# Two transformer blocks on one core: the first block's down-projection turned to token rows with 512 columns, and twelve products of constants ahead of the second up-projection

## The reference, cut to what matters

```python
def first_block(x, ...):
    ...
    x = x + mixed @ w_out[l]
    u = _rmsnorm(x, g_mlp[l]) @ w_ff1[l]
    x = x + jnp.square(jax.nn.relu(u)) @ w_ff2[l]      # 4096 -> 1024
    return x

def second_block(x, ...):
    u = rmsnorm(h, norm_mix_pre_w[layer])
    proj = u @ w_in[layer]                             # q, k, v first
    ...
    h = h + rmsnorm(mixed, norm_mix_post_w[layer])
    f = rmsnorm(h, norm_ffn_pre_w[layer])
    f = jnp.square(jax.nn.relu(f @ w_up[layer])) @ w_down[layer]
    h = h + rmsnorm(f, norm_ffn_post_w[layer])
    return h
```

## Time and profile before

| | |
|---|---|
| runs of the kernel before | 1190.92 us, three times the same |
| the profiled execution's own time | 1192.29 us |
| its span, first to last instruction | 1190.5 us |
| TensorE (PE) busy | 99% of the span |
| VectorE (DVE) busy | 70% |
| ScalarE (ACT) busy | 56% |
| GpSimdE (POOL) busy | 1% |
| mean granted TensorE clock | 0.998 |
| read from memory | 210.87 MB, 178 GB/s over the span |

### The profile page before, as it was taken

The page is one execution under the profiler, slowest core; times in us unless marked ns, Lnnn a source line. Parts: engine busy times, 40 slices in busy tenths (PEclk is TensorE's granted clock), DMA queues, the critical chain, the costliest instruction groups (busy, mean ns, idle before and its releaser), DMA issues.

```text
span 1190.5 us, 19559 instructions
## 1 busy us (share of the span) xinstructions
PE 1179.1 (99%) x8398; PEld 1105.6 (93%) x8398; DVE 829.2 (70%) x952; ACT 664.2 (56%) x766; POOL 16.4 (1%) x34
## 2 busy tenths in 40 slices
PE   9999999999999999999999999999999999999998
PEld 8999999999888899999999999999988888999886
DVE  7867676787756567776547758999987557677543
ACT  7543545677553445544434558889885435555342
POOL 0000000000000000000000000000000000000000
PEclk9999999999999999999999999999999999999999
DMA  9553445556665645556564746556456644555651
GB/s 328 166 172 108 148 146 166 152 159 182 212 218 192 207 148 165 189 178 213 177 186 153 233 123 202 179 172 197 162 191 234 205 149 160 167 173 186 219 204 43
DMA packets 181269, 213.23 MB, mean 179 GB/s; under 512 B 6700, under 2 KB 147372, under 8 KB 181184
## 3 DMA queue, kind: packets, MB, share of 16 engines
q1 hardware_dynamic: 177696, 200.30, 52.5%
q0 software_dynamic: 2912, 10.79, 3.0%
q10 hardware_dynamic: 576, 0.90, 0.2%
HBM read 210.87 MB, written 1.09 MB: 178 GB/s over the span
## 4 chain that ended last, share of the span: by engine, by line
PE 87%; DVE 9%; ACT 3%; issue 1%; DMA 0%; DVEq 0%; ACTq 0%
PE ps L242 50%; PE ps L2013 20%; PE ps L2342 7%; PE ps L1764 5%; DVE w_lo L210 3%; DVE arena L1270 3%; PE ps L1813 1%; PE ps L1767 1%; ACT w_hi L204 1%; DVE arena L1593 1%; PE ps L2302 1%; DMA pcol<-in_params 0%; DVE arena L1609 0%; PE ps L2309 0%; DVE arena L1625 0%
## 5 line engine op out<-in xcount | busy, mean ns | idle before, releaser
L210 DVE TENSOR_TENSOR w_lo<-raw,w_hi 128x2048 fp32r<-128x2048 f32 x187 | 428.0, 2290 | 195.6 <-ACT w_hi L204 195.3
L242 PE MATMUL ps<-x_hi,w_hi 128*128 128x256 f32 x1760 | 506.5, 288 | 0.0
L242 PE MATMUL ps<-x_hi,w_lo 128*128 128x256 f32 x1760 | 498.3, 283 | 0.0
L242 PE MATMUL ps<-x_lo,w_hi 128*128 128x256 f32 x1760 | 498.2, 283 | 0.0
L204 ACT CAST w_hi<-raw 128x2048 fp32r<-128x2048 f32 x187 | 354.8, 1901 | 195.1 <-PE ps L2013 101.9
L242 PEld LDWEIGHTS ps<-x_hi,w_hi 128*128 128x128 f32 x1760 | 337.6, 192 | 4.0 <-issue 3.0
L242 PEld LDWEIGHTS ps<-x_lo,w_hi 128*128 128x128 f32 x1760 | 337.7, 192 | 0.7
L242 PEld LDWEIGHTS ps<-x_hi,w_lo 128*128 128x128 f32 x1760 | 337.5, 192 | 0.0
L2013 PE MATMUL ps<-w_hi,x_hi 128*128 128x512 f32 x344 | 135.1, 393 | 0.0
L2013 PE MATMUL ps<-w_lo,x_hi 128*128 128x512 f32 x344 | 134.0, 390 | 0.0
L2013 PE MATMUL ps<-w_hi,x_lo 128*128 128x512 f32 x344 | 134.0, 390 | 0.0
(11 more groups left out here) (244 smaller groups left out, 1193.7 us busy)
## 6 DMA issues: line engine op xcount, KB each, us to landing
raw<-in_w_in SPq DMA_DIRECT2D x170, 512.0 KB, 4.7
raw<-in_w_ff SPq DMA_DIRECT2D x64, 512.0 KB, 4.5
raw<-in_w_up SPq DMA_DIRECT2D x32, 512.0 KB, 4.3
raw<-in_w_down SPq DMA_DIRECT2D x32, 512.0 KB, 4.6
raw<-in_w_mem_kv SPq DMA_DIRECT2D x16, 512.0 KB, 6.1
raw<-in_w_out SPq DMA_DIRECT2D x16, 512.0 KB, 4.3
raw<-in_w_ssm_proj SPq DMA_DIRECT2D x16, 512.0 KB, 4.6
raw<-in_w_x_proj SPq DMA_DIRECT2D x8, 512.0 KB, 4.8
```

What stands on the lines that cost most here:

```text
L210: nc.vector.tensor_tensor(w_lo[:, s], raw[:, s], w_hi[:, s].bitcast(FP32), ALU.subtract)\
L242: last = nc.tensor.matmul(dst, l, r, start=start and k == 0 and m == 0, stop=stop and k == nk - 1 and m == 2)
```

## The change

The down-projection of the first block is computed like that of the second: `down` has 16 units of 4 pieces by 512 columns, 24 products of 512 columns each, tokens on the partitions. The units 0 to 7 give output features 0 to 511 in banks 3 and 4 (one for each half of the tokens), the units 8 to 15 features 512 to 1023 in banks 5 and 6. ACT copies the finished banks to `mixt` (`down_copy`), PE turns them back in 128 x 128 transposes (`down_turn`, 8 inside unit 9's end, 8 more between parts of q and k), DVE adds them to `res` from the turned banks 0, 1, 3, 4 (`down_added`). q's and k's products are reordered around the turns, q's second output tile goes to bank 0, and v, which uses bank 0 too, is preceded by a wait for DVE having taken q. The loads become two DMAs of 2 pieces by 512 columns. Apart from that, twelve products of the matrix of ones with itself (128 columns) go to PE ahead of `with_high(0)`, and DVE does `post_added(0)` ahead of `post_scaled(1)`.

```diff
@@ -317,6 +317,9 @@
         def y_bank(c, t):
             return bank(3 + c * 2 + t, 512)
 
+        def down_turned(p):
+            return bank(p if p < 2 else p + 1, 2, T)
+
         def wide(w):
             return w.rearrange("p k n -> p (k n)").rearrange("p (k n) -> p k n", k=4)
 
@@ -405,7 +404,8 @@
                     wide_load(gate_unit(s, 2 + n), wp, 4 * n, s % 2 * 512)
             plain("out", a["w_out"][0], 4)
             plain("up", a["w_ff1"][0], 16)
-            deep("down", a["w_ff2"][0])
+            for b in range(16):
+                wide_load(U("down", b), a["w_ff2"][0], b % 8 * 4, b // 8 * 512)
 
             for i in range(3):
                 for n, c in enumerate((AQ, AK, AV)):
@@ -826,19 +826,34 @@
                     act.wait_ge(S("f_sq"), c + c0 + 1)
                     A(rows(x_hi, 2 * c + U0, 2), cells(1024 + 512 * (c % 2), 2, T), ACT.Copy).then_inc(S("f_hi"), 1)
 
-            def deep(dst, done0, stop, g=None):
-
-                for b in range(16):
-                    if b < stop:
-                        split()
-                    if b % 4 == 3:
-                        act.wait_ge(S(f"deep{b // 4 % 2}"), b // 8 + done0 + 2)
-                        if g is not None:
-                            high(dst, g, b // 4, H0, "b_hi")
-                        squares(dst, b // 4 * 2)
+            def down_copy(c, t):
+
+                A(mixt[:, t, y_cols(c)], y_bank(c, t), ACT.Copy).then_inc(S("d_copy"), 1)
+
+            def down_high(p):
+
+                act.wait_ge(S(f"deep{p % 2}"), 2 + p // 2)
+                high(res, "norm_mix_pre_w_2", p, H0, "b_hi")
 
             hidden("up", 0)
-            deep(res, 0, 16, "norm_mix_pre_w_2")
+            for b in range(16):
+                split()
+                if b == 8:
+                    finished(act, U("down", 7))
+                    down_copy(0, 0)
+                    down_copy(0, 1)
+                if b == 11:
+                    for p in (0, 1):
+                        down_high(p)
+                        squares(res, 2 * p)
+            act.wait_ge(S("d_half"), 1)
+            down_copy(1, 0)
+            finished(act, U("down", 15))
+            down_copy(1, 1)
+            down_high(2)
+            down_high(3)
+            squares(res, 4)
+            squares(res, 6)
             split()
             inverse(1)
             for b in range(4):
@@ -1481,24 +1496,31 @@
                         split()
                     low(2 * c + U0, q, "f_hi", c + c0 + 1, "f_lo")
 
-            def deep(stage, dst, add, n, stop, g=None):
-
-                for b in range(16):
-                    if b < stop:
-                        split()
-                    if b % 4 == 3:
-                        c = b // 4
-                        finished(dve, U(stage, b))
-                        d, v = rows(dst, 2 * c, 2), ps[:, 3 + c % 2 * 2:5 + c % 2 * 2, 0:T]
-                        last = tt(d, d, v, ALU.add) if add else V.tensor_copy(d, v)
-                        last.then_inc(S(f"deep{c % 2}"), 1)
-                        if g is not None:
-                            lower(dst, g, c, 0, H0, ("b_hi", "b_lo"))
-                        pair(n, c)
+            def down_added(p):
+
+                dve.wait_ge(S("d_t"), max(p, 1))
+                d = rows(res, 2 * p, 2)
+                tt(d, d, down_turned(p), ALU.add).then_inc(S(f"deep{p % 2}"), 1)
+
+            def down_low(p):
+
+                lower(res, "norm_mix_pre_w_2", p, 0, H0, ("b_hi", "b_lo"))
 
             dve.wait_ge(S("n_r"), 1)
             hidden("up", 0)
-            deep("down", res, True, 1, 16, "norm_mix_pre_w_2")
+            for b in range(16):
+                split()
+                if b == 11:
+                    for p in (0, 1):
+                        down_added(p)
+                        down_low(p)
+                        pair(1, p)
+            down_added(2)
+            down_added(3)
+            down_low(2)
+            down_low(3)
+            pair(1, 2)
+            pair(1, 3)
             split()
 
 
@@ -1559,7 +1581,11 @@
             for n, dst in enumerate((a_q, a_k)):
                 u = U("att", 0, n, 3)
                 finished(dve, u)
-                tt(dst, unit_bank(u), bc(rs_row(), 2), ALU.mult).then_inc(taken(u), 1)
+                if n == 0:
+                    tt(dst[:, 0], unit_bank(u)[:, 0], rs_row(), ALU.mult)
+                    tt(dst[:, 1], bank(0, T), rs_row(), ALU.mult).then_inc(taken(u), 1)
+                else:
+                    tt(dst, unit_bank(u), bc(rs_row(), 2), ALU.mult).then_inc(taken(u), 1)
             split()
             split()
             step_sizes()
@@ -1717,9 +1743,11 @@
             dve.wait_ge(S("n_r"), 3)
             post_scaled(0)
             for k in range(KT):
-                if k + 1 < KT:
+                if 0 < k < KT - 1:
                     post_scaled(k + 1)
                 post_added(k)
+                if k == 0:
+                    post_scaled(1)
                 if k > 1:
                     post_low(k - 2)
             post_low(KT - 2)
@@ -2072,18 +2100,31 @@
                 if b == 3:
                     last.then_inc(S("n_ss"), 1)
 
-            def deep(stage, done0):
-
-                for b in range(16):
-                    u, c = U(stage, b), b // 4
-                    begin(u)
-                    pe.wait_ge(S("f_lo"), 8 * done0 + 4 * (b % 4 + 1))
-                    if b % 4 == 0:
-                        pe.wait_ge(S(f"deep{c % 2}"), c // 2 + done0 + 1)
-                    for o in range(2):
-                        last = products(pe, u, o, U0 + KT * (b % 4), FP, out_=bank(3 + c % 2 * 2 + o, T),
-                                        start=b % 4 == 0, stop=b % 4 == 3)
-                    last.then_inc(S(f"unit{u % SLOTS}"), 1)
+            def down_turn(h, tokens):
+
+                for t in tokens:
+                    pe.wait_ge(S("d_copy"), 2 * h + t + 1)
+                    for k in range(4):
+                        last = tr(down_turned(2 * h + k // 2)[:, k % 2, t * P:(t + 1) * P],
+                                  mixt[:, t, (4 * h + k) * P:(4 * h + k + 1) * P])
+                        if t == 1 and k in ((3,), (1, 3))[h]:
+                            last.then_inc(S("d_t"), 1)
+
+            def down(b):
+
+                u, c = U("down", b), b // 8
+                begin(u)
+                pe.wait_ge(S("f_lo"), 2 * (b % 8 + 1))
+                for t in range(2):
+                    for k in range(4):
+                        for m, (wt, xt) in enumerate(((w_hi, x_hi), (w_hi, x_lo), (w_lo, x_hi))):
+                            last = nc.tensor.matmul(y_bank(c, t), xt[:, U0 + 4 * (b % 8) + k, t * P:(t + 1) * P],
+                                                    wide(wt[:, u % SLOTS])[:, k],
+                                                    start=b % 8 == 0 and k == 0 and m == 0,
+                                                    stop=b % 8 == 7 and k == 3 and m == 2)
+                    if b == 15 and t == 0:
+                        last.then_inc(S("d_half"), 1)
+                last.then_inc(S(f"unit{u % SLOTS}"), 1)
 
             u, v = U("out", 0), U("out", 1)
             outs = (unit_bank(u)[:, 0], bank(0, T))
@@ -2110,7 +2151,10 @@
             norm(0, 3)
             for i in range(1, 16):
                 unit(U("up", i), H0)
-            deep("down", 0)
+            for b in range(16):
+                down(b)
+                if b == 9:
+                    down_turn(0, (0, 1))
 
 
             def step_sizes():
@@ -2159,11 +2203,22 @@
                 last.then_inc(S("soft_y"), 1)
 
             q, k, v = (U("att", 0, n, 3) for n in range(3))
-            half(q, 0, H0, lo=("b_lo", 0, 1))
+            late = ("b_lo", 0, 1)
+            begin(q)
+            pe.wait_ge(S("deep1"), 2)
+            products(pe, q, 0, H0, FP, 4, stop=False, lo=late)
+            down_turn(1, (0,))
+            begin(k)
+            products(pe, k, 0, H0, FP, 4, stop=False)
+            down_turn(1, (1,))
+            products(pe, q, 1, H0, FP, 4, out_=bank(0, T), stop=False)
+            products(pe, q, 0, H0, FP, lo=late, k0=4)
             norm_folded(1)
             norm(1, 3)
-            half(q, 1, H0)
-            unit(k, H0)
+            products(pe, q, 1, H0, FP, out_=bank(0, T), k0=4).then_inc(S(f"unit{q % SLOTS}"), 1)
+            products(pe, k, 0, H0, FP, k0=4)
+            products(pe, k, 1, H0, FP).then_inc(S(f"unit{k % SLOTS}"), 1)
+            evacuated(pe, q)
             half(v, 0, H2, TOK, lo=("n_lo", KT, 1))
             step_sizes()
             half(v, 1, H2, TOK)
@@ -2313,6 +2368,8 @@
 
             begin(U("up2", 0))
             begin(U("up2", 1))
+            for _ in range(12):
+                mm(first[1][2][:, 0:P], ones, ones)
             with_high(0)
             for k in range(1, KT):
                 with_high(k)
```

(3 more changed lines are left out.)

## The result

The changed kernel takes **1194.63 us** (median of 8 runs, 1194.43 to 1195.63); the kernel before, measured with it, 1192.28 us (8 runs, 1190.92 to 1192.52). The ratio is 1.0026, with a 95% interval of 1.0017 to 1.0035: slower by 3.1 us, 2.0 to 4.2 (it is taken over all runs; the medians alone lie 2.35 apart, since three of the eight runs of before stood at 1190.92). The profiled execution of the changed kernel took 1194.64 us with a span of 1192.8, against 1192.29 and 1190.5 before. The forecast was 1192.8, and "within 0.2%" was its likeliest class; the measurement lies in the range and on the slower side, just beyond that bound. Two executions of a later kernel (e3) ran slow from end to end, at 1433.94 and 1932.61 us with mean granted clocks of 0.753 and 0.556, and are left out of its numbers.

The account below looks back on a forecast made before the run. PE, busy 99% of the span, was taken as the bound. -5.2 + 0.9 + 6.3 + 1.6 - 1.7 = +1.9 us takes 1192.29 to 1194.2; less the 1.4 between profiled execution and median, 1192.8, range 1187.5 to 1195.5.

Parts of the forecast that it names:

- within 0.2%: Whole kernel: no change a measurement can tell, between 1188.5 and 1193.3 us; chance 0.50.
- Down-projection, -5.2: First block's `down`: 384 products of 512 columns replace 768 of 256, saving 5.2 us on PE.
- the first turns, +0.9: First eight turns inside PE's stream at unit 9 of `down`: 0.88 us added.
- 4.4 us for sixteen: All sixteen turns at the Trainium skill's about 275 ns each: 4.4 us instead of 1.8.
- Start of `att`, +6.3: Start of `att`: PE idles 4.5 us for DVE's taking of q; v begins 18.7 after q, not 12.4.
- The small waits I put at 1.1: Inside q and at the norm's sums in `att`: PE waits some 1.1 us for low parts and pairs.
- The clock behind the wait, +1.6: After PE's idle time in `att`: 3.2 us at half clock lose 1.6 us; bounds 0 and 3.2.
- Ahead of `up2`, -1.7: Second up-projection: twelve products of ones fill PE's 2.9 us wait and keep the clock full, saving 1.7 us.
- the third rival: In `att`: clock stays low twice as long, another 1.6 us, 1194.4 to 1195.4 us; chance 0.13.
- That the clock holds in `att`: Rival: no fall of the clock after the wait in `att`, 1.6 us less, 1191.2 us; chance 0.15.
- That DVE reaches q in time: Rival at the start of `att`: v's wait under 1 us, total -4.0, 1186.9 to 1188 us; chance 0.15.
- The fourth: Rival in `down`: wide products no cheaper per column, the 5.2 us gone, 1198.0 us; chance 0.02.

Follow-up runs that it names:

- e3: Kernel before plus only twelve products of ones ahead of the second up-projection and first addition ahead of second scaling: 1190.78 us, ratio 0.9991.
- e1: Changed kernel with q's second output tile in bank 5 instead of bank 0: 1189.35 us, ratio to before 0.9977.
- e7: Changed kernel, bank 0 and the wait kept, with DVE taking q ahead of the scaling for v: 1190.04 us, ratio 0.9982.
- e2: Changed kernel with 18 products of ones ahead of v's wait, bank 0 and the wait kept: 1193.19 us, ratio to before 1.0012.
- e5: Changed kernel with q's second tile in bank 5, without the twelve products of ones: 1190.78 us.
- e12: Same kernel as e5, run once more for a profile; the two profiles of that kernel are at 1190.80 and 1189.69 us.
- e11: Kernel before, unchanged, for a second profile: 1190.92, 1191.01, five runs from 1192.17 to 1192.54, and 1193.44 us.
- e4: Changed kernel without the twelve products and with the old order of scaling and adding: 1196.18 us, ratio to before 1.0037.
- e6: Changed kernel with q's second tile in bank 5 and the second scaling back ahead of the first addition: 1189.50 us.
- e8: Changed kernel with q's second tile in bank 5 and DVE's step-size weights ahead of its split of v's weights: 1189.06 us, ratio 0.9974.

## Why the prediction was right, and where it was off

**Down-projection, -5.2, and the first turns, +0.9: right.** Forecast 88.0 us with the turns, measured 87.96 (543.28 to 631.24), 4.2 less than before. The rate of the second down-projection carried over; nothing that was costed at nothing showed in PE's waits there. Each turn lasts 0.27 us in the trace, but the next begins 0.11 behind it: the forecast rightly added distances, while its 4.4 us for sixteen adds up durations.

**Start of `att`, +6.3: right in mechanism and in size.** v began 18.65 after q, forecast 18.7, so +6.3. The step-by-step times held: DVE's split at 9.0 (forecast 8.9), q's taking at 17.8 (17.8, though its own terms, 8.9 and 8.82, make 17.7). v began 0.06 behind the end of DVE's second half (649.67 to 649.73) where I had put 0.14. The view has a wait of 4.1 for the 4.5, but it counts from the modelled end of the product before; from start to start it is 4.3, since PE could have begun v at 14.4 instead of 14.2. The small waits I put at 1.1 show as 0.2 and 0.3 for the same reason: 14.4 less 96 products, two sums and eight turns (11.5, 0.9, 0.9) leaves 1.1. e1 and e7 each removed the cause and got the time back.

**The clock behind the wait, +1.6: right.** The first half of v took 1.7 us too long, and e2 gave back 1.4 by filling the wait.

**Ahead of `up2`, -1.7: right for the execution it was read from, and only for that.** From the start of the norm's sums after `out2` to that of the next sums, behind the first tiles, the traces have 996.29 to 1013.74 before and 1000.28 to 1016.07 after: 17.45 and 15.79, a gain of 1.7.

**The sum.** -4.2 + 6.3 + 1.6 - 1.7 = +2.0 for the profiled executions; their spans differ by 2.3, of which 0.33 arose at the very start, where the up-projection began at 456.70 instead of 456.37 after a first load of 5.10 us instead of 4.75. That part is no effect of the change: the start varied from execution to execution of one kernel, by 0.12 (before, 456.37 and 456.49) and 0.37 (bank 5 without ones, 456.58 and 456.95).

**The step that failed is the last one: "The runs' median, 1190.92, lies 1.4 below the profiled execution, so I forecast 1192.8."** I took that offset for a property of profiling and carried it over. It was the fall of the clock itself. The profiled execution had suffered it (0.50 in the earlier trace rows), the three runs shown had not; for these that is inferred, from the mean clock of 0.999 in every run of before at that level and from the pair of profiles of e5 and e12. For a run without the fall there is nothing for the twelve products to give back: its sum is -5.2 + 0.9 + 6.3 + 1.6 and about -0.1 for the order, +3.5, which from 1190.92 gives 1194.4. The changed kernel measured 1194.43 to 1194.89 in six of eight runs. With the fall the sum is +1.9, which from 1192.3 gives 1194.2, the same. So the terms themselves give 1.4 to 1.6 more than the 1192.8 that I wrote, and the measured median lies 1.8 above it; with that went the choice of the likeliest class, "same" instead of "slower". That the time still lies in the range is owed to the width of the range. It also lies between 1194.4 and 1195.4, the price of the third rival, by coincidence: the profiled run, at 1194.64, had only one stretch at half clock. e5, e11 and e12 show the two kinds of run.

**The rivals.** That the clock holds in `att` was wrong: it would show as runs 1.6 below the others, and none is. That DVE reaches q in time was wrong, but was made true by the bank in e1: that kernel is 3.0 under the median of before (1192.34 to 1189.35), so the rival's gain of 4.0 was 1.0 too large. Its +2.0 up to v held (14.4 against 12.4). What it left out are v's late low parts and the thin products' wait of 0.3: from v's start to these it was 3.6 there instead of 3.0. Of the other 0.4, 0.2 is the later start of the kernel and 0.1 the down-projection. That the clock stays low twice did occur: two of the eight runs stood 0.5 us or more above the other six (1195.44 and 1195.63, with mean clocks of 0.996), and e4's profile shows such a run from inside, 6.4 us at half after the same wait. The first part of that stretch cost nothing, as PE was idle, so the price was 0.9 to 1.0 and not 1.6. The fourth was wrong, as the row of the same loop had said.

## What to carry to other kernels

When an accumulator is put into the bank that a later step uses, look not at when its products end but at when the engine that empties it gets to it in its own order: here v could have begun 4.3 us earlier, as it did in e1, and PE stood 4.1 us for a read that DVE did last. A bank that has just been emptied, or that read put first, was worth 5 us, more than the whole gain of the wider products. And when the runs of one kernel stand at levels that are further apart than their scatter, ask first at which level the profiled run stood before adding a term from the profile to a median of the runs.

## What the runs showed of the hardware that was not expected

After an idle stretch of 2.7 or 2.9 us TensorE's clock falls to half in some executions of the same program and not in others: the two profiles above, 0.50 and 1.00 over the same 3.2 us. After an idle stretch of 4.1 us it fell in both profiles that have one (the changed kernel and e4). Kernels that had such a wait and no filling stood at levels 1.2 to 1.5 us apart: before 1190.9, 1192.4 and 1193.6; bank 5 without ones 1189.3, 1190.8 and 1192.2. The clock stayed at half for about 3.2 to 3.4 us in these profiles, with one exception: 6.4 us behind e4's wait of 4.1, although PE was busy without a break in the last 5.3 of them; the longer stretch came with the upper level of that kernel. The kernels with both waits filled or gone (e1, e6, e8) kept all their runs within 0.6 us. So the twelve products ahead of the up-projection gain nothing over the best run of a kernel without them; they take away the chance of the worse ones.
